# Layer ends of a two-layer decoder trunk on one core: statistics by block, halves, columns in another order, half of the result through TensorE

## The reference

```python
h = layer_norm(x, ln_in_g, ln_in_b)
for l in range(DEPTH):
    mix = hybrid_mixer(h, w_in[l], w_out[l], ...)
    h = layer_norm(DEEPNORM_ALPHA * h + mix, ln_mix_g[l], ln_mix_b[l])
    ffn = grouped_moe(h, w_router, router_bias, w_gate[l], w_up[l], w_down[l])
    h = layer_norm(DEEPNORM_ALPHA * h + ffn, ln_ffn_g[l], ln_ffn_b[l])
return h
```

## Time and profile before

| | us |
|---|---|
| three runs | 658.54, 659.53, 658.72 |
| the profiled execution: its time | 658.54 |
| its span, first to last instruction | 656.7 |
| TensorE busy | 640.2 (97%) |
| DVE, ScalarE, POOL busy | 306.2, 188.0, 126.3 |

### The profile page before, as it was taken

The page is one execution under the profiler, slowest core; times in us unless marked ns, Lnnn a source line. Parts: engine busy times, 40 slices in busy tenths (PEclk is TensorE's granted clock), DMA queues, the critical chain, the costliest instruction groups (busy, mean ns, idle before and its releaser), DMA issues.

```text
span 656.7 us, 7900 instructions
## 1 busy us (share of the span) xinstructions
PE 640.2 (97%) x3208; PEld 346.1 (53%) x3208; DVE 306.2 (47%) x598; ACT 188.0 (29%) x373; POOL 126.3 (19%) x118
## 2 busy tenths in 40 slices
PE   7999999999999999999999999999999999999994
PEld 5887786553333443333478888764433344333331
DVE  6598797821232220320548969884032140320326
ACT  3721863241110220101183277341310113100101
POOL 1997000700000000000069940024000000000001
PEclk9999999999999999999999999999999999999998
DMA  9991199899999999999997037988999999999991
GB/s 364 431 379 64 55 431 426 323 430 429 428 425 427 431 427 428 426 428 428 430 427 306 1 112 284 429 377 360 430 428 427 427 428 429 424 430 427 424 415 72
DMA packets 18330, 240.79 MB, mean 367 GB/s; under 512 B 2032, under 2 KB 2160, under 8 KB 3440
## 3 DMA queue, kind: packets, MB, share of 16 engines
q1 hardware_dynamic: 17136, 234.46, 84.6%
q10 hardware_dynamic: 1152, 5.77, 2.3%
HBM read 239.17 MB, written 1.05 MB: 366 GB/s over the span
## 4 chain that ended last, share of the span: by engine, by line
PE 82%; DVE 9%; DMA 5%; ACT 2%; issue 1%; POOL 0%; DVEq 0%
PE bank L649 31%; PE bank L670 16%; PE bank L541 12%; PE bank L698 5%; DMA ring<-in_units 5%; PE bank L762 4%; DVE w_split L1298 3%; PE bank L622 2%; PE bank L515 2%; PE bank L602 2%; PE bank L471 2%; PE bank L582 1%; PE bank L529 1%; PE bank L659 1%; DVE h L1338 1%
## 5 line engine op out<-in xcount | busy, mean ns | idle before, releaser
L649 PE MATMUL bank<-ring,xe 128*64 128x512 f32 x1024 | 223.6, 593 | 0.3 <-DMA ring<-in_units 0.3
L649 PEld LDWEIGHTS bank<-ring,xe 128*64 128x64 f32 x1024 | 74.4, 137 | 142.9 <-issue 140.1
L670 PE MATMUL bank<-ring,area_b 128*64 128x512 f32 x512 | 113.8, 596 | 0.2
L1497 DVE TENSOR_TENSOR area_b<-area_b,bank 128x512 f32<-128x512 f32 x16 | 11.0, 687 | 209.2 <-PE bank L649 209.2
L1143 POOL TENSOR_TENSOR rstd<-var_eps,half_neg 128x1 f32<-128x1 f32 x18 | 11.9, 665 | 490.5 <-DVE var_eps L1246 490.5
L1172 POOL TENSOR_TENSOR in_lo<-ring,in_hi 128x512 fp32r<-128x512 f32 x60 | 75.8, 1313 | 9.8 <-ACT in_hi L958 9.7
L670 PEld LDWEIGHTS bank<-ring,area_b 128*64 128x64 f32 x512 | 35.2, 137 | 66.7 <-issue 64.9
L1517 DVE SCALAR_TENSOR_TENSOR y_lo<-bank,slot_gate,y_hi 128x512 fp32r<-128x512 f32 x32 | 24.0, 751 | 85.0 <-ACT y_hi L1041 85.0
L1027 ACT ACTIVATE area_b<-bank 128x512 f32<-128x512 f32 x16 | 9.6, 597 | 163.4 <-PE bank L649 163.4
L1041 ACT ACTIVATE y_hi<-bank,slot_gate 128x512 fp32r<-128x512 f32 x32 | 22.0, 687 | 96.4 <-PE bank L670 96.4
L541 PE MATMUL bank<-in_hi,xi_hi 128*128 128x512 f32 x120 | 47.5, 396 | 0.0
(11 more groups left out here) (181 smaller groups left out, 737.6 us busy)
## 6 DMA issues: line engine op xcount, KB each, us to landing
ring<-in_units SPq DMA_DIRECT2D x109, 2048.0 KB, 23.2
ln_par<-in_ln_rows ACTq DMA_DIRECT2D x4, 1024.0 KB, 8.9
ring<-in_units SPq DMA_DIRECT2D x2, 1024.0 KB, 8.1
h<-in_x SPq DMA_DIRECT2D x2, 512.0 KB, 4.1
piece_area<-in_branch_rows ACTq DMA_DIRECT2D x2, 512.0 KB, 4.9
ln_par<-in_ln_rows SPq DMA_DIRECT2D x1, 1024.0 KB, 35.8
piece_area<-in_sgw_cols ACTq DMA_DIRECT2D x2, 256.0 KB, 5.1
out<-h SPq DMA_DIRECT2D x1, 512.0 KB, 2.7
```

The lines of the kernel that those rows point to most:

```text
L649: mm = pe.matmul(bank[2 + m][e * SLOTS:(e + 1) * SLOTS, :], xe[:, k, at + e * SLOTS:at + (e + 1) * SLOTS], w[:, c, m, e, :], start=k == 0, ...
L670: mm = pe.matmul(bank[5 + n][e * SLOTS:(e + 1) * SLOTS, :], hidT[:, k, e * SLOTS:(e + 1) * SLOTS], w[:, k, e, :], start=k == 0, stop=k == ...
```

## The change

**Start and turn.** The centred rows are made in halves of 512 columns, each with a signal of its own (`input_center`, `input_ready`), and TensorE turns each half as it comes. ScalarE and DVE read the columns out in a mixed order of blocks (`ACT_COLUMNS`, `DVE_COLUMNS`), and the first pass of the slab takes chunks 0, 1, 4, 5, 2, 6, 3, 7. `sum_rows` moves behind the first pass. The clock matmuls are 10 and not 12 at the turn, and three more stand at the start.

**Layer end.** Where no extra rounds are due, DVE aggregates block 0 before it takes the statistics of block 1; this stands inside a branch, whose other side holds the extra rounds.

**Tail.** Rows of block 0 get scale and shift from TensorE: ScalarE makes a diagonal matrix of the block's rstd, TensorE puts the shift into two banks (identity times shift) and adds diagonal times (centred rows times gain); ScalarE copies the banks to `h`. DVE makes only the product with the gain there, in halves, and block 1 as before but in four halves. SP stores four halves, block 0 first.

```diff
-KEEP_START, KEEP_ROUTER, KEEP_SLOTS, KEEP_TURN = 14, 18, 6, 12
+KEEP_START, KEEP_ROUTER, KEEP_SLOTS, KEEP_TURN = 14, 18, 6, 10
+KEEP_FIRST = 3
...
+ACT_COLUMNS = ((0, 0), (0, 1), (1, 0), (1, 1), (0, 2), (1, 2), (0, 3), (1, 3))
+DVE_COLUMNS = ((0, 4), (0, 5), (0, 6), (1, 4), (1, 5), (0, 7), (1, 6), (1, 7))
+SLAB_CHUNKS = (0, 1, 4, 5, 2, 6, 3, 7)
...
+        diagonal = area_b[:, 512:512 + P]
...
-            sp.wait_ge(result_ready, 1)
-            sp.dma_start(out[0, 0:P, :], h[:, 0, :]).then_inc(out_done, 16)
-            for n in range(2):
-                half = slice(n * BANK, (n + 1) * BANK)
-                sp.wait_ge(result_ready, n + 2)
-                sp.dma_start(out[0, P:2 * P, half], h[:, 1, half]).then_inc(out_done, 16)
-            sp.wait_ge(out_done, 16 * 3)
+            for b in range(TB):
+                for n in range(2):
+                    half = slice(n * BANK, (n + 1) * BANK)
+                    sp.wait_ge((rows_out, result_ready)[b], n + 1)
+                    sp.dma_start(out[0, b * P:(b + 1) * P, half], h[:, b, half]).then_inc(out_done, 16)
+            sp.wait_ge(out_done, 16 * 4)
...
-            def turn(src, b):
+            def turn(src, b, ready=None):
                 for half in range(2):
+                    if ready is not None:
+                        pe.wait_ge(input_ready, ready + half + 1)
...
-                    pe.wait_ge(norm_ready, 2 * TB * l + b + 1)
-                    turn(normal, b)
-                if l == 0:
-                    sum_rows()
+                    turn(normal, b, 2 * TB * l + 2 * b)
                 w = unit_at(u0).rearrange("p (h c n) -> p h c n", h=2, c=KC)
                 for k in (2, 3, 0, 1):
                     if l == 0 and k == 2:
                         pe.wait_ge(first_half_in, 16)
                     elif k == (2, 0)[l == 0]:
                         wait_unit(pe, u0)
-                    for n in range(KC):
-                        c = n // 2 + 4 * (n % 2)
-                        if k == 2:
-                            pe.wait_ge((tr_act, tr_dve)[n % 2], (TR_ACT, TR_DVE)[n % 2] * l + 4 * (TB - 1) + n // 2 + 1)
+                    for n, c in enumerate(SLAB_CHUNKS):
+                        if k == 2 and c < 4:
+                            pe.wait_ge(tr_act, TR_ACT * l + columns_made(ACT_COLUMNS, TB - 1, c))
+                        elif k == 2:
+                            pe.wait_ge(tr_dve, TR_DVE * l + columns_made(DVE_COLUMNS, TB - 1, c))
                         mm = pe.matmul(bank[4 + k // 2][:, (k % 2) * SEQ:(k % 2 + 1) * SEQ],
                                        w[:, 1 - k // 2, c, (k % 2) * P:(k % 2 + 1) * P], xT[:, c, :], start=n == 0, stop=n == KC - 1)
+                    if l == 0 and k == 2:
+                        sum_rows()
...
+            def result_rows():
+                pe.wait_ge(par_in, 16 * (2 * DEPTH + 1))
+                for n in range(2):
+                    pe.matmul(bank[n][:, :], ident, ln_par[:, 1, n * BANK:(n + 1) * BANK], start=True, stop=False)
+                pe.wait_ge(rows_kept, TB * DEPTH + 1)
+                for n in range(2):
+                    pe.wait_ge(norm_ready, TB * DEPTH + n + 1)
+                    pe.matmul(bank[n][:, :], diagonal, h[:, 0, n * BANK:(n + 1) * BANK], start=False, stop=True)\
+                      .then_inc(proj_pe, 1)
...
                 if l == DEPTH - 1:
                     with pe.If(n > SLOTS):
                         more_rounds(l)
+                    result_rows()
                     return
...
+            keep_clock(6, KEEP_FIRST)
             layers_from(0)
...
+            def scaled_columns(l):
+                for b, c in ACT_COLUMNS:
+                    act.wait_ge(tr_pe, 12 * l + 2 * b + 1)
+                    act.activation(xT[:, c, b * P:(b + 1) * P], bank[2 * b][:, c * P:(c + 1) * P],
+                                   ACT.Identity, scale=col_par[:, 2 * l, 0, c:c + 1],
+                                   bias=col_par[:, 2 * l, 1, c:c + 1]).then_inc(tr_act, 1)
...
+            act.wait_ge(ln_rstd, n_ln - 1)
+            act.activation(diagonal, ident, ACT.Copy, scale=rstd[:, n_ln - 2:n_ln - 1]).then_inc(rows_kept, 1)
+            for n in range(2):
+                act.wait_ge(proj_pe, DEPTH + n + 1)
+                act.activation(h[:, 0, n * BANK:(n + 1) * BANK], bank[n][:, :], ACT.Copy).then_inc(rows_out, 1)
...
+            def input_center(i, src, b):
+                dve.wait_ge(ln_rstd, i + 1)
+                for half in range(2):
+                    at = slice(half * BANK, (half + 1) * BANK)
+                    dve.tensor_scalar(normal[:, b, at], src[:, at], mv[:, b, 0:1], rstd[:, i:i + 1], ALU.subtract, ALU.mult)\
+                       .then_inc(input_ready, 1)
...
-                if ps.main:
-                    for b in range(TB):
-                        nth("comb", pairs - 1, 3 + b, 4)
-                        dve.bn_stats(stats[:, b, 1, :], bank[LAST_COMB_BANKS[2 + b]][:, :]).then_inc(s["stats"], 1)
-                else:
+                if not ps.main:
...
+            def last_stats(l, b):
+                main = passes[l][0]
+                dve.wait_ge(main.s["comb"], 4 * PAIRS * (l + 1) - 1 + b)
+                dve.bn_stats(stats[:, b, 1, :], bank[LAST_COMB_BANKS[2 + b]][:, :]).then_inc(main.s["stats"], 1)
...
-                with dve.If(n > SLOTS):
+                counts = steps[0], norms[0]
+                with dve.If(n <= SLOTS):
+                    norm = []
+                    for b in range(TB):
+                        last_stats(l, b)
+                        dve.wait_ge(main.s["stats"], 4 * l + 3 + b)
+                        norm.append(norm_variance(b, 2))
+                with dve.Else():
+                    steps[0], norms[0] = counts
+                    for b in range(TB):
+                        last_stats(l, b)
                     dve.wait_ge(rows_kept, TB * (l + 1))
...
-                dve.wait_ge(main.s["stats"], 4 * (l + 1))
-                norm = [norm_variance(b, 2) for b in range(TB)]
-                dve.wait_ge(rows_kept, TB * (l + 1))
+                    dve.wait_ge(main.s["stats"], 4 * (l + 1))
+                    norm = [norm_variance(b, 2) for b in range(TB)]
                 if l < DEPTH - 1:
                     for b in range(TB):
-                        norm_center(norm[b], acc[:, b, :], b)
+                        dve.wait_ge(rows_kept, TB * l + b + 1)
+                        input_center(norm[b], acc[:, b, :], b)
                 else:
                     dve.wait_ge(par_in, 16 * (2 * l + 3))
-                    norm_apply(norm[0], acc[:, 0, :], h[:, 0, :], 0, ln_par[:, 0, :], ln_par[:, 1, :], result_ready)
-                    step(dve.scalar_tensor_tensor(out=h[:, 1, :], in0=acc[:, 1, :], scalar=mv[:, 1, 0:1], in1=ln_par[:, 0, :],
-                                                  op0=ALU.subtract, op1=ALU.mult))
+                    for b in range(TB):
+                        dve.wait_ge(rows_kept, TB * l + b + 1)
+                        for n in range(2):
+                            half = slice(n * BANK, (n + 1) * BANK)
+                            dve.scalar_tensor_tensor(out=h[:, b, half], in0=acc[:, b, half], scalar=mv[:, b, 0:1],
+                                                     in1=ln_par[:, 0, half], op0=ALU.subtract, op1=ALU.mult).then_inc(norm_ready, 1)
                     dve.wait_ge(ln_rstd, norm[1] + 1)
                     for n in range(2):
                         half = slice(n * BANK, (n + 1) * BANK)
+                        dve.wait_ge(norm_ready, TB * DEPTH + TB + n + 1)
...
```

45 lines of the change are left out of this document (20 added, 25 removed).

## The result

The changed kernel took 661.27 us (median of 16 executions, 660.06 to 662.28), the kernel before 658.93 (16 executions): ratio 1.003, interval 1.002 to 1.004. It is slower by 2.3 us. The forecast was 658.8, with a range up to 660.0: it was wrong. The profiled execution took 661.15 us with a span of 659.4, against 658.54 and 656.7, so 2.7 us have to be found. (Executions of the kernel before lie in three groups, at about 658.4 to 659.4, 659.5 to 660.7 and 661.7 to 662.7 us, with a mean granted clock of 0.996, 0.994 and 0.991 of full; so its median differs from one set of runs to the next, and I compare ratios, or distances inside the traces.) One execution each of the kernel before (738 us), of stats_plain (2,360 us) and of jump_after (948 us) lies far off all others; they count in no ratio, and no trace shows what happened in them.

A forecast was written before the change was run, and what follows sets the result against it. Almost all of the span was taken as TensorE's unchanged matmuls, so only start, turn and tail count: -0.05 - 1.0 + 1.1 = +0.05 us on 658.54, or 658.8 on the median, range 656.7 to 660.0.

The forecast's parts named there:

- Start: Before layer 0's slab: earlier slab start wins 0.9 us, router's sums now in the open lose 0.85; -0.05.
- Turn: Between the layers: earlier statistics and centring in halves start layer 1's slab sooner, all passed to the end; -1.0 us.
- Rival D: Turn between the layers: its gain is lost to a TensorE wait for weights near 629 us; 659.8 us, chance 0.05.
- Tail: After the last matmuls: block 0's result rows wait for TensorE's 3.7 us jump, and the stores queue; +1.1 us.
- What would show it: Trace signs: right if slabs, a 3.7 us tail branch and ScalarE's late copy match; wrong if the branch is below 1 us.
- C: Tail: TensorE fetches code twice, a second 3.7 us gap between shift products and diagonal; 662.5 us, chance 0.08.
- E: Tail: the eight new matmuls run at the lower clock, +0.6 to +1.2; 659.4 to 659.9 us, chance 0.05.

The follow-up runs named there:

- stats_plain: shifts_first with the last layer's statistics in the old order (both blocks' sums, then both aggregations, no Else part on VectorE); 657.38 us, 0.9967 of the kernel before.
- jump_after: stats_plain with TensorE's shifts and result rows in the branch entered without a jump, so one far jump follows them and none precedes; 659.56 us.
- whole_blocks: stats_plain with the centring of start and turn in whole blocks again instead of halves; 658.50 us.
- stats_never: stats_plain with the old order of statistics at the turn between the layers too; 657.79 us, 0.9968 of the kernel before.
- turn_only: The changed kernel with the tail of the kernel before, so start and turn alone; 658.68 us, 0.9981 of the kernel before.
- rows_behind: The changed kernel with TensorE's result rows moved behind the outer branch, so no second far jump follows them; 660.45 us, 1.0011 of the kernel before.
- shifts_first: rows_behind with TensorE's shift products issued ahead of layer 1's branch; 658.13 us, 0.9972 of the kernel before.
- tail_only: The kernel before with the new tail alone, its statistics as they were; 662.99 us, 1.0063 of the kernel before.
- jump_late: The kernel before plus one TensorE wait ahead of the outer branch's jump, which makes a second far jump; 660.36 us.
- wait_alone: The kernel before plus the same TensorE wait as jump_late, but behind the outer branch, so no second jump follows; 659.14 us.

## Why the prediction was wrong, step by step

The sum in the profiled executions: layer 0's last combining matmul +0.18, turn -0.90, layer 1 -0.10, tail +3.51; together +2.69, which is the span's 2.7.

**Start, forecast -0.05 (-0.3 to +0.2): right in size, though what passes on is not settled at the slab.** The slab's end moved by -0.15 (25.66 to 25.51). By the end of layer 0 this was +0.18. POOL's power of block 1 was done 1.03 us behind the start of the centring, between the working's 0.89 (in after the first half) and 1.29 (after the second), and nearer the first. Over the fourteen traces the last matmul of the first slab starts between 24.83 and 25.70, layer 0's last combining matmul between 326.59 and 327.27, and up to 25.33 the one says nothing of the other: 24.83 led to 326.59, 25.28 to 326.60 and to 327.08. Between them lie waits for the weight stream; the changed kernel's list of TensorE's waits from 60 to 327 us has one that the earlier trace rows gave no hint of:

```profile
PE bank L661 <- DMA ring<-in_units: 0.3, 1, 0.3
```

The premise that "whatever brings TensorE forward before 445 us brings the stream forward too" is too strong for layer 0.

**Turn, forecast -1.0 (-1.3 to -0.4): right, measured -0.90, and kept to layer 1's end (-0.10 more).** The size is in part luck: the working has the centring start 2.0 us behind the last combining matmul, and it starts 2.28 behind it, as VectorE has block 1's variance 0.1 later and its jump leaves a gap of 0.14 and not 0.06; from there to the slab it takes 2.81 us, the better end of the 2.8 to 3.15 of the working. Its parts, if they add: 0.37 from the halves (whole_blocks), 0.16 from the statistics' order (stats_never), and the rest, 0.37, is left to the columns' order and the fewer clock matmuls, which were not tried alone. The power of block 1 got in beside VectorE's centring (0.65 us, for up to 1.32 in the earlier trace rows). Rival D, which lost this gain to the stream, did not come.

**Tail, forecast +1.1 (+0.8 to +1.4): wrong, measured +3.5.** Its first half is right. The branch took 3.8 us, the shifts stood behind it, and the last store's issue moved by 1.04 where the working says 0.9. Two things in it were off: the products on VectorE start 0.7 late and not 0.1 (turn_only), which costs nothing, as TensorE's 3.0 us of delay covers it; and the last two stores go out 0.89 us behind the one before them (653.57 to 654.46) and not 0.70, which is the rest of the 1.04. The step that failed is the next sentence: "Three stores of 256 KB then stand in one line ... each further one costs 0.6 when they queue. Last landing at 657.2 to 657.7". With four stores that have the DMA engines to themselves, the landing is 2.6 us after the issue (rows_behind, shifts_first, stats_plain), so the queueing costs 0.5, the forecast's upper end. What it put at nothing is a second far jump behind the result rows, whose code packet moves among the stores: 2.0 us more in the profiled execution (4.58 for 2.60), 0.8 by the medians and 1.2 by the ratios. Without that jump (rows_behind) the loss is 0.7 us by the ratio, inside the forecast's range. None of the signs under "What would show it" looked past the last store's issue, and so all of those for "right" came out: slab, turn, branch of 3.8 us, shifts behind it, ScalarE's second copy 6.7 us behind the last combining matmul. Rivals with this size were not on the list: C had TensorE fetch twice, but priced the second fetch as a wait of TensorE between the shifts and the products (662.5), and asked where a code block ends. Nobody waits for the second fetch on TensorE; the stores do, on the DMA engine that carries it.

Both facts for it stood in the rows. The earlier trace rows has the packet that comes after the jump has ended, at 7.5% of 16 engines over 1 us, which is 1.2 us of one engine; I read it only as a sign that the next block comes unasked. And the outer If/Else of `layers_from` needs a jump over its Else part; in the earlier trace rows it was missing since it had been merged with the inner one. The Trainium skill ("Runtime: NRT & Kernel Launch", section "Instruction fetch mechanics") says that each engine's sequencer fetches code in blocks of 16 KiB through its own DMA queue, and that crossing a block costs a mostly hidden tail-bump. The traces agree with the blocks and the queue (q8, 16 KB a packet). That it is hidden holds for TensorE in straight code: before, two such packets move between 460 and 500 us, where TensorE is busy 39.97 of 40. It did not hold for the stores that needed the same DMA engine.

**E, the clock in the tail (0.05): not in the profiled execution, but in another kernel's.** The granted clock was 1.00 until 654.7. tail_only shows it at 0.63, with 1.7 us on TensorE's eight matmuls; the groups of rows_behind would fit it, untraced.

What holds for the changed kernel's whole loss, in the traces: rows_behind removes 2.2 us of the landing's distance to the last combining matmul (12.82 to 10.61), shifts_first another 0.97 by hiding the jump, stats_plain another 0.64. The tail is then 0.31 shorter than before's, as the edit of the tail meant, and with the turn the kernel is 0.33% faster than before.

Open: which DMA engine carries a code packet, and so how much of the stores it delays in a given execution. The profiled delays go from 0.3 us (tail_only) over 0.5 (jump_late, jump_after) to 2.0 (the changed kernel), the medians' differences from 0.8 (the changed kernel over rows_behind) over 1.2 (jump_late over wait_alone) to 2.2 (jump_after over stats_plain), and these hold differences of the clock too. Where the lower clock in the later groups of the kernel before sits was not traced; turn_only, shifts_first, stats_never and whole_blocks have no such groups, each with twelve executions within 1.2 us.

## What to carry to other kernels

A far jump can cost more than the engine's own stall: its code is carried by the same DMA engines as the data, and one packet in the wrong microsecond makes a store wait that spans all of them (0.3 to 2.0 us in these traces). So put work that is to follow a branch where the jump is already made, or the jump where no one stores; and when code is put between the ends of two nested branches, count the jumps again. Let the engine have work in its queue ahead of the jump (the shifts here), which hides the stall; with it the executions at a lower clock were gone too.

## What the runs showed of the hardware that was not expected

- A far jump of TensorE took 3.3 to 4.1 us in fourteen traces, and moved two 16-KB packets, one 0.9 to 1.0 us after it began (1.4 in wait_alone) and one 0.6 to 0.8 us after it ended (1.9 in jump_after). Where the packets of two jumps met (jump_late), they came 1.0 to 1.2 us after either point, and the second jump took 5.04 us. A packet held its engine for 0.9 to 2.0 us, a 2-KB packet of the result for 0.084.
- A jump of VectorE has a record of 47 to 72 ns, but 0.50 us pass in the changed kernel's tail before the next instruction starts, and 0.14 at the turn. Why they differ stays open.
- TensorE idle for 2.15 us was followed by a clock of 0.63 (tail_only), idle for 2.59 and 2.37 us by 1.00 (the changed kernel, rows_behind): the length of the idle time alone does not decide.
- Four stores of 256 KB, issued 0.4 to 0.9 us apart, land 2.60 us after the last issue, in six traces within 0.01; where only two 256-KB stores end the program, 2.11.
